# The output projection of a hybrid encoder layer in groups of seven products, on one core

## The reference

```
h = rmsnorm(x) * norm_w
proj = h @ w_in                       # 8192 columns and 16 gate columns
q_a, k_a, v_a, z_a = 4 x 1024 columns # 8 heads of dilated attention, QK-norm, partial rotary
q_m, k_m, v_m, o_m, z_m               # 4 heads of a two-way mLSTM, chunkwise
attn = attention(q_a, k_a, v_a) * silu(z_a)
hm = sigmoid(o_m) * rmsnorm(mlstm(q_m, k_m, v_m, gates)) * silu(z_m)
out = x + concat(attn, hm) @ w_out    # 2048 x 2048
```

## Time and profile before

| | |
|---|---|
| median of 3 runs | 2039.66 us (2037.93 to 2040.56) |
| profiled execution, its own time | 2038.74 us |
| its span, first to last instruction | 2036.9 us |
| PE busy | 1984.6 us of it |
| DVE, ACT, POOL busy | 1282.5, 837.5, 192.6 us |
| mean granted clock of PE | 0.996 |

### The profile page before, as it was taken

The page is one execution under the profiler, slowest core; times in us unless marked ns, Lnnn a source line. Parts: engine busy times, 40 slices in busy tenths (PEclk is TensorE's granted clock), DMA queues, the critical chain, the costliest instruction groups (busy, mean ns, idle before and its releaser), DMA issues.

```text
span 2036.9 us, 27050 instructions
## 1 busy us (share of the span) xinstructions
PE 1984.6 (97%) x9257; PEld 1623.8 (80%) x9257; DVE 1282.5 (63%) x2649; ACT 837.5 (41%) x1342; POOL 192.6 (9%) x188
## 2 busy tenths in 40 slices
PE   4999999899999999999999999999999999999999
PEld 3887788788888888888887878778777787788887
DVE  7777757768768768767766576575766544443222
ACT  5553325435435335334453343635537344251110
POOL 4340000110010010010000111010111000000000
PEclk8999999999999999999999999999999999999999
DMA  4673326474464365366457665364546625415443
GB/s 157 209 272 137 115 99 198 113 161 124 115 161 129 100 177 143 104 156 149 121 176 259 163 156 125 88 153 96 136 119 161 227 74 191 160 63 193 142 152 108
DMA packets 160231, 299.35 MB, mean 147 GB/s; under 512 B 17456, under 2 KB 36432, under 8 KB 157792
## 3 DMA queue, kind: packets, MB, share of 16 engines
q1 hardware_dynamic: 140128, 259.87, 38.8%
q0 software_dynamic: 19968, 37.76, 12.1%
HBM read 194.67 MB, written 102.90 MB: 146 GB/s over the span
## 4 chain that ended last, share of the span: by engine, by line
PE 88%; DVE 4%; DMA 3%; issue 3%; ACT 1%; SPq 0%; POOL 0%; DVEq 0%; ACTq 0%; POOLq 0%
PE ps L732 18%; PE ps L734 18%; PE ps L736 18%; PE ps L760 5%; PE ps L762 5%; PE ps L761 5%; PE ps L942 3%; PE ps L911 3%; PE ps L880 1%; PE ps L836 1%; PE ps L845 1%; PE ps L928 1%; DMA arena<-rot_dram 1%; PE ps L839 1%; PE ps L946 1%
## 5 line engine op out<-in xcount | busy, mean ns | idle before, releaser
L732 PE MATMUL ps<-t_hi,w_hi 128*128 128x512 f32 x1792 | 716.4, 400 | 42.2 <-DVE t_lo L1677 12.6
L734 PE MATMUL ps<-t_lo,w_hi 128*128 128x512 f32 x1792 | 701.5, 391 | 0.0
L736 PE MATMUL ps<-t_hi,w_lo 128*128 128x512 f32 x1792 | 701.1, 391 | 0.0
L732 PEld LDWEIGHTS ps<-t_hi,w_hi 128*128 128x128 f32 x1792 | 338.3, 189 | 123.6 <-issue 57.8
L736 PEld LDWEIGHTS ps<-t_hi,w_lo 128*128 128x128 f32 x1792 | 338.4, 189 | 72.0
L734 PEld LDWEIGHTS ps<-t_lo,w_hi 128*128 128x128 f32 x1792 | 338.9, 189 | 65.7
L978 ACT CAST w_hi<-w_raw 128x512 fp32r<-128x512 f32 x256 | 158.4, 619 | 391.4 <-PE ps L736 195.3
L1214 DVE TENSOR_TENSOR w_lo<-s_tmp,w_hi 128x512 fp32r<-128x512 f32 x256 | 182.4, 712 | 135.3 <-ACT w_hi L978 126.0
L1214 DVE TENSOR_TENSOR w_lo<-w_raw,w_hi 128x512 fp32r<-128x512 f32 x256 | 181.8, 710 | 133.9 <-ACT w_hi L978 127.5
L978 ACT CAST w_hi<-s_tmp 128x512 fp32r<-128x512 f32 x256 | 158.6, 619 | 239.9 <-PE ps L736 228.9
L760 PE MATMUL ps<-t_hi,w_hi 128*128 128x512 f32 x384 | 154.1, 401 | 5.5 <-DVE xt L1668 5.4
(11 more groups left out here) (217 smaller groups left out, 2657.0 us busy)
## 6 DMA issues: line engine op xcount, KB each, us to landing
w_raw<-w_all_dram SPq DMA_DIRECT2D x320, 256.0 KB, 3.8
fin_dram<-xt SPq DMA_DIRECT2D x128, 256.0 KB, 4.2
fin_dram<-xt POOLq DMA_DIRECT2D x128, 256.0 KB, 4.6
arena<-fin_dram SPq DMA_DIRECT2D x64, 512.0 KB, 7.3
arena<-xT_dram SPq DMA_DIRECT2D x44, 256.0 KB, 6.0
arena<-xT_dram SPq DMA_DIRECT2D x16, 512.0 KB, 4.3
arena<-rs_dram SPq DMA_DIRECT2D x16, 512.0 KB, 7.2
y_raw<-y_dram SPq DMA_DIRECT2D x16, 512.0 KB, 4.7
```

Of the source, the lines that this page charges most:

```text
L732: nc.tensor.matmul(ps[:, bank, :], hi, t_hi[:, n, k, :], start=new and k == 0, stop=False, skip_group_check=True)
L734: nc.tensor.matmul(ps[:, bank, :], hi, t_lo[:, n, k, :], start=False, stop=False, skip_group_check=True)
L736: mm = nc.tensor.matmul(ps[:, bank, :], lo, t_hi[:, n, k, :], start=False, stop=k == KP - 1, skip_group_check=True)
```

## The change

The output projection becomes 16 more groups of the same kind (`GROUPS` has 80, units 448 to 559): eight with the mLSTM's half of the contraction (stage 3, from unit 448), eight with attention's (stage 4, from unit 504). `out_product`, `output`, `residual`, `part_dram` and the `y_high`/`y_low` of before are gone. The residual: SP copies x to the output in DRAM at 16 even steps from unit 45 on (`FILL_AT`), and POOL's adding transfers put each block of the projection on top. The moving side needs sums of y blocks: DVE makes those of the mLSTM from three and one more loads of y at units 325 to 327 and 342 (`ym_loads`, `ym_sums`), those of attention per head at offset 22 (`ya_sums`), both through `ty_dram`. SP then asks for one 1 MB block per operand straight into `t_lo` (`ym_operands` from unit 442, `ya_loads` from 498), ACT casts it to `t_hi`, and DVE subtracts in place (`y_low`), at units 444 to 450 and at 500, 502 to 507. `A_START` is 357 + 17h; a head's loads of v and z move from offsets 4 and 6 to 8 and 9. At the start the additions `t_three` and `t_four` of stage 0 go from POOL to DVE, the scaling of the first x block from DVE to ACT, and the order of the first loads changes; some steps of the gates are spread over more units (59 to 69 before, 61 to 79 now).

```diff
-          + [(M_PAIRS + p, 0) for p in range(A_PAIRS)])
+          + [(M_PAIRS + p, 0) for p in range(A_PAIRS)]
+          + [(M_PAIRS + A_PAIRS + p, kh) for kh in range(2) for p in range(O_PAIRS)])
-A_START = [357 + 18 * h for h in range(ATT_HEADS)]
+A_START = [357 + 17 * h for h in range(ATT_HEADS)]
+Y_SPLIT = {3: {n + 3: n for n in range(PRODUCTS)}, 4: {3: 0, 5: 1, 6: 2, 7: 3, 8: 4, 9: 5, 10: 6}}
+FILL_AT = 45
+YM_AT = 321
...
+                if odd == 0 and 0 <= i < O_TILES:
+                    sp.dma_start(outT[i], xT[i]).then_inc(filled, 16)
...
+            def ym_operands(off):
+                if 1 <= off <= PRODUCTS:
+                    sp.wait_ge(prod, PRODUCTS * (STAGE[3] - 1) + off)
+                    y_there(sp, 3, off - 1)
+                    sp.dma_start(t_lo[:, off - 1].bitcast(F32), y_block(3, off - 1)).then_inc(t_in[off - 1], 16)
...
+                if off == 0:
                     sp.wait_ge(m_out, 16 * M_HEADS)
+                    sp.dma_start(ym_a, y[:, 0:KP, 0:HALF]).then_inc(ym_in, 16)
+                    sp.dma_start(ym_b, y[:, 0:KP, HALF:]).then_inc(ym_in, 16)
+                    sp.dma_start(ym_c, y[:, KP:, HALF:]).then_inc(ym_in, 16)
...
+            def y_low(b, off):
+                n = Y_SPLIT[b].get(off)
+                if n is not None:
+                    dve.wait_ge(th_done[n], t_made(n, b))
+                    nc.vector.tensor_tensor(t_lo[:, n], t_lo[:, n].bitcast(F32), t_hi[:, n].bitcast(F32), ALU.subtract
+                                            ).then_inc(tl_done[n], 1)
...
+            def ya_sums(h):
+                low, high = ystage[:, 0:HALF], ystage[:, HALF:]
+                dve.wait_ge(a_y, 4 * h + 4)
+                if h < KP:
+                    dve.wait_ge(a_pv, 4 * h + 4)
+                    nc.vector.tensor_tensor(y_sums[:, 0, :], high, low, ALU.subtract).then_inc(ya_sum, 1)
+                    return
+                dve.wait_ge(ya_in, 32 * (h - KP + 1))
+                nc.vector.tensor_tensor(y_sums[:, 1, :], high, y_sums[:, 1, :], ALU.subtract).then_inc(ya_sum, 1)
+                nc.vector.tensor_tensor(y_sums[:, 0, :], high, y_sums[:, 0, :], ALU.subtract).then_inc(ya_sum, 1)
+                dve.wait_ge(ya_sum, sums_of_y(h) + 1)
+                nc.vector.tensor_tensor(y_sums[:, 2, :], low, y_sums[:, 1, :], ALU.subtract).then_inc(ya_sum, 1)
```

More of the change, by code:

```diff
@@ L29 @@
 O_TILES = D_MODEL // P
+O_PAIRS = O_TILES // 2
 EPS = 1e-6
@@ L82, in stores_of, with t_loaded, sums_of_y @@
     return sum(accumulated(i) == added for i in range(g, -1, -step))
-LAST_STORE = (NG - 2, NG - 1, NG - 2, NG - 1, NG - 1, NG - 1)
-PLAIN = [stores_of(x, LAST_STORE[x], False) for x in range(6)]
+KEPT = (1, 3, 4, 5)
+SUMS = (3, 1, 5, 4)
 def t_made(n, b):
-    return (4 if n < 2 else 1) + b
-KEPT = (1, 3, 4, 5)
+    return (4 if n < 2 else 1) + b - int(b >= 2 and n in KEPT)
+def t_loaded(n, b):
+    return 32 * (n in KEPT) + (16 * (b - 2) + 16 * (b == 4 and n == 1) if b > 2 else 0)
+def sums_of_y(h):
+    return h if h < KP else KP + 3 * (h - KP)
 def chunk_of(n):
@@ L101, in prepared_in, with build_program @@
 def prepared_in(u):
-    if u + 2 < IN_UNITS:
-        return u + 2
-    v = u + 2 - IN_UNITS
-    return IN_UNITS + v // 2 if v % 2 == 0 and v < O_UNITS else None
-def last_unit_of(block):
-    return block if block < IN_UNITS else IN_UNITS + 2 * (block - IN_UNITS) + 1
-def build_program(nc, xT, w_all, w_gates, vecs, norm_cols, m_cols, att_mask, rope, eye, tri, fin, part, y_dram, t_dram, eps_dram, rows_dram, rs_dram,
+    return u + 2 if u + 2 < UNITS else None
+def build_program(nc, xT, w_all, w_gates, vecs, norm_cols, m_cols, att_mask, rope, eye, tri, fin, y_dram, t_dram, ty_dram, eps_dram, rows_dram, rs_dram,
                   rot_dram, outT):
@@ L256, in build_program @@
         t_out = sem("t_out")
-        t_in = [sem(f"t_in{n}") for n in KEPT]
+        t_in = [sem(f"t_in{n}") for n in range(PRODUCTS)]
         c_ncol = sem("c_ncol")
@@ L625, in _ @@
                 x_block(0, B11, kt)
+            for kt in range(KP):
+                x_block(0, B12, kt)
             weights(0, 1, 0, 0)
@@ new lines, in _ @@
+                if g + 1 < NG:
+                    next_weights(g, n)
+                plain_stores(g, n)
+                gate_loads(u)
+                gate_stores(u)
+                i, odd = divmod(u - FILL_AT, 2)
+                if odd == 0 and 0 <= i < O_TILES:
+                    sp.dma_start(outT[i], xT[i]).then_inc(filled, 16)
+                for j in range(M_HEADS):
+                    mlstm_loads(j, u - M_START[j])
+                ym_loads(u - YM_AT)
+                t_stores(u)
```

409 lines of the change are left out of this document (168 added, 241 removed).

## The result

The changed kernel takes 2051.39 us (median of 6 runs, 2048.39 to 2052.47) against 2040.11 us of the kernel before beside it (6 runs): ratio 1.005, 95% interval 1.0039 to 1.0061. It is slower by half a per cent, where the forecast was faster by 0.8%. The profiled execution has a span of 2050.5 us, 13.6 more than before, and a mean clock of 0.986 (before 0.996).

The account below looks back on a forecast made before the run. PE, busy 97% of the span, was taken to bound the kernel. Terms -43.5 + 8.6 + 7.0 + 4.0 + 2.3 + 2.0 + 2.5 + 0 = -17.1 gave 2021.6 us profiled, median 2022.5, range 2005 to 2036.

Parts of the forecast that it names:

- Two of its signs: Prediction wrong if DVE does not end the waits at the named places, or heads 1 to 4 wait over 1 us more.
- Fewer units: Whole kernel: 128 units become 112, at 2.72 us each on PE, 43.5 us less.
- mLSTM's sums: Units 325 to 327: three DVE subtractions in a row and late loads cost 4.0 us, bounds 0 and 8.
- Heads every 17 units: Heads: closeness alone free; colliding sums and rotations, rotated-row waits, less v and z crowding: +2.3 us, bounds -5 and +12.
- The rival that ended at 2050: Heads 1 to 7 each wait 6 us on DVE for rotated rows and broadcasts; change ends 10 us slower; chance 0.05.
- Stage 3: Units 444 to 451: DVE over-asked by operand splits, plus waits, 13.6 us; less 5.0 going away, net +8.6.
- 5.0 us that were to go away: Around stage 3: PE waits of 0.7 and 3.2 us before the old output's evictions, with restarts, vanish.
- Stage 4: Units 500, 502 to 507: DVE over-asked, and operand 1's last quarter some 3 us late: +7.0 us, bounds 2 and 13.
- The end: After the last matmul: eviction, then a POOL transfer of 0.88 us to issue and 4.6 to land: +2.5 us.
- The start: Start: stage 0's last operand ready at about 51 us as before, effect 0, bounds -5 and +3.
- The rival by which the start gains 5 us: Start: removing POOL's work, if that alone held it back, gains 5 us, ending at 2017.5; chance 0.09.
- Clock: New waits in the three places: one or two long enough for the clock to drop, +2.0 us.

Follow-up runs that it names:

- Experiment 1: Changed kernel with DVE, at a head's offset 12, copying the transposed values first and multiplying z afterwards: 2042.0 us, ratio 1.001 to the kernel before.
- experiment 12: Kernel before with heads every 17 units, v and z asked for at offsets 8 and 9 and multiplied at 10 and 12: 2068.15 us, ratio 1.0127.
- experiment 5: Changed kernel with stage 3's seven operand loads asked for by ACT's queue in place of SP's, each once its product is done: 2045.69 us, ratio 1.0016.
- experiment 7: Changed kernel with ACT asking for stage 3's operands and DVE subtracting only a quarter of each low part: 2041.9 us, ratio 1.0007.
- Experiments 4, 5 and 6: Changed kernel, stage 3: a quarter of DVE's subtractions, 2050.81 us; loads asked for by ACT, 2045.69 us; a quarter of each operand loaded, 2049.52 us.
- experiment 8: Changed kernel with the last quarter of stage 4's operand 1 sent from SBUF to SBUF, not through DRAM: 2051.94 us, ratio 1.0045.
- Experiment 2: Changed kernel with the old start: POOL makes t_three and t_four, DVE scales the first x block, old load order: 2048.75 us, ratio 1.0041.

## Why the prediction was wrong, step by step

The prediction named what would show it wrong. Two of its signs came in part: heads 1 to 3 have new waits of 1.5 to 2.2 us each before their transposes (line 903) and head 4 one of 1.0, and at the largest wait of stage 3 the releaser is not DVE but ACT.

*Fewer units: right.* A plain unit takes 2.72 us in the new stages too, so the 227 ns for one matmul that the prediction took from the trace are what 192 of them were worth. The 131 ns that the Trainium skill states (TensorE: Matmul & The Clock Gate, Back-to-back issue gap) do not hold for this stream.

*mLSTM's sums: right*, 3.3 for 4.0, in the units named.

*Heads every 17 units: the step that failed by most*, 13.5 us for 2.3. "Bringing heads closer alone costs nothing" was argued from DVE's busy share, and the part looked at rotated rows and at offset 22 and 5. The waits for rotated rows fell, as it had said for v and z, from 25.0 to 8.2 us. What it did not ask is what the moved multiplications now stand ahead of: it counted what their loads leave free, not the place of the work. At offset 12 PE waits for the next DVE instruction at once, and the 2.0 us of lag that the prediction allows evictions do not exist. Experiment 1 gives 8 to 10 of the 11 us, and experiment 12 shows the same wait in the kernel before. The rival that ended at 2050 had the right time with the wrong mechanism, which is luck: its waits for rotated rows did not come.

*Stage 3: right place, half the cause.* The sum of 39 us of DVE work against 26 of PE gave 13.6 before what goes away, and with the loads in time (experiment 5) the excess is 13.0. That the two agree is luck in part: with 11 us of that work taken away as well (experiment 7) only 2.6 us go, where the sum would give nearly all. DVE has no gap from 1590 to 1610 us, as forecast, and its evictions end the waits before units 448 and 449. But in the changed kernel another chain ended later: SP's queue, and behind the last load ACT's cast and ACT's eviction. The forecast had put "waits" at 2.6 us for DMA by its bandwidth. It had not read what stands ahead of `ym_operands` on SP, though it stands in the code: a head's loads that wait for the end of the head before, later by a unit and a half than before, and for the last operand the next group's weights, which wait for a sum of DVE. Experiments 4, 5 and 6 show that it is the queue: less DVE 0.6 us, fewer bytes 2.5, another queue 7.5. That the spacing delayed it is argued from the code. Of the 5.0 us that were to go away there 3.9 did. With both mends 10.4 stayed; the late broadcast accounts for 4.3 of them and the eviction before unit 449 for 3.1. The rest, about 3 us, is not placed; the clock is at half for 3.4 us behind the second wait.

*Stage 4: mis-sized*, 11.8 for 7.0, of which the prediction's own steps give only 5.5. The chain over the last quarter of operand 1 was the wrong one (experiment 8). DMA is full for 30 us (share 1.01, 329 GB/s) and carries 4.7 us, DVE 3.0; 7.3 and 9.0 us are left when one of them is taken away alone, and what both together would leave was not run, so some 4 us of this stage have no cause shown.

*The end: mis-sized*, 6.8 for 2.5. The landing was as forecast (3.8 us after the issue); that the span waits for POOL's queue to drain, 5 us longer, was in no row that the prediction read. In the kernel before POOL's last transfer is issued at 1770.0 us and its drain, until 1777.8, lies beside other work.

*The start: wrong*, 3.9 for 0, outside its upper bound of 3 in this trace and about at it in the mean of the traces. The last low part of stage 0 was to be ready at about 51 us as before; it is done at 52.9, before at 50.6. The rival by which the start gains 5 us when POOL's additions go did not come in. By the Trainium skill (SBUF — State Buffer, Who interferes with whom) a DVE instruction with two SBUF inputs contends with a GpSimd instruction that reads SBUF; the trace agrees in so far as the subtraction that took 3.11 us beside POOL takes 2.29 us now. That DVE took over more than it got back is a reading and not shown, since the orders of scaling and loads changed too. Experiment 2 puts unit 7 back.

*Clock:* 2.0 forecast; what it cost stands in the rows of the table, with the clock at half from 1606.9 to 1613.7 and from 1624.0 to 1630.8 us, beginning within PE's waits of 4.6 and 5.1 and lasting into the products behind them.

Apart from the first two and the clock, which has no figure of its own, every term was too small, mostly for work that had come to stand behind something else. A sum of such terms needs an upper end that adds them; the range to 2036 did not. The prediction's own upper bounds added up (15, 13, 8, 12 and 3 us, with 2.0 and 2.5 for the clock and the end, against 43.5) come to some 12 us over the kernel before, which is where the result lies.

## What to carry to other kernels

When an edit moves an instruction or a request, list what stands directly behind it on its engine and its queue, and how much lag the consumer of that has: 1.2 us of DVE ahead of a copy that PE wants at once cost 8 to 10 us in eight heads, and two waits on an in-order queue made unrelated loads up to 13 us late. Where a stretch is over-asked on one engine, test which chain ends last before mending: taking away 11 us of DVE's work changed nothing that could be seen, and 2.6 us once the loads came in time. A smaller count of matmuls (43.5 us here) is worth its price only with the feeding mended; then the same change gives 2020 to 2028 us (ratios 0.9905 to 0.9928).

## What the runs showed of the hardware

- The end of a program whose last transfer is POOL's adding one comes 9.0 us after its issue (2041.55 to 2050.5), though it lands after 3.8. In all 18 traces POOL's closing drain lasts 7.8 to 9.1 us from its last transfer; it only shows where nothing else runs that long. With a plain store by SP last the end comes 2.8 us after the issue (2038.42 to 2041.2).
- A load of 1 MB asked for alone landed in 4.8 us (at 1572.08). Four asked for within 7 us beside weights and stores, at 337 GB/s, took 5.2, 5.8, 9.8 and 15.3 us.
- An engine's own queue couples unlike work: ACT stood 8.1 us before a cast whose load was late, and the eviction behind it kept PE idle for 5.1 us.
